# A pitch of 520 words in place of 512 for the rows of a weight ring in SBUF

## The chip, the cores and the metric

The kernel runs on one core of a Trainium2 chip. The metric is the time of one execution on the device in microseconds (us). A profile is one execution taken by the hardware profiler; its span runs from the first to the last instruction.

## The reference

One decoder layer for a sequence of 256 tokens at width 2048, in float32. Cut to what is computed:

```python
h    = rms_norm(x, ln_mix_w)
proj = h @ w_in                                   # 2048 x 9216
u_pool, q, f_logit, inp, g, gate_a, gate_b = split(proj)
y_a  = multiscale_pool(u_pool, pool_mix_w, pool_scale) @ w_branch_a
y_b  = hgrn2(q, f_logit, inp, g, lb, hgrn_norm_w) @ w_branch_b   # 8 heads, chunks of 64
x    = x + (sigmoid(gate_a) * y_a + sigmoid(gate_b) * y_b) @ w_out
u    = causal_depthwise_conv(rms_norm(x, ln_ffn_w) @ w_up, conv_w, conv_b)   # 2048 x 11008
u_gate, u_val = split(u)
x    = x + (silu(u_gate) * u_val) @ w_down        # 5504 x 2048
x    = x + sigmoid(rms_norm(x, ln_ple_w) @ w_ple_gate) * (p @ w_ple)
out  = rms_norm(x, ln_final_w)
```

## The kernel before

Nearly all the work is products of the 256 tokens with large weight matrices. A float32 product is made of three float32r ones: each operand is split into a high part (what a copy to float32r keeps) and a low part (the rest), and hi*hi + hi*lo + lo*hi is accumulated in PSUM.

**Units and the ring.** The weights stream from HBM in units of two row tiles of 128 x 512 words, 508 units in all, in the order of the stages: the projection w_in (q, f, i, g twice, the pool columns), then per 512 output columns the two gates of w_in, w_branch_a and w_branch_b (the merge), then w_out, w_up (22 chunks, the last one narrow, with a convolution behind each), w_down (43 row tiles, so that the last unit of each chunk has one), w_ple and w_ple_gate (the gate stage). Unit u goes through slot u % 4 of a ring of RING = 4 slots that three arrays share: `raw` (as it came), `w_hi` and `w_lo`. Each array is [128 partitions, 4 slots, 2 rows, 512 words].

- SP issues the DMA into `raw` (`rows`, L364; for w_up two DMAs of 2 x 256 words, L372 and L373) as soon as DVE has finished with the unit four before (`slot_split`).
- ACT copies `raw` to `w_hi` (`split_hi`, L737) three units ahead of PE (LEAD), once PE has finished the unit that held the slot.
- DVE subtracts, `w_lo` = `raw` - `w_hi` (`split_lo`, L941).
- PE takes the unit (`unit`, L504 to L518): for each of the two rows a, for each of the two blocks of 128 tokens, three matmuls. The stationary operand is 128 x 128 of the activations, the moving one is a row of the ring, 512 words.

Units of w_up's last chunk use 2 x 256 words of each row pair; in the ring copies that is five units (`width_of`).

**The stationary operands** are xT_hi and xT_lo for w_in, w_up and w_ple_gate; yaT and obT for the two branches; mT for w_out; aT for w_down; pT for w_ple. **Layout:** SBUF tensors are allocated in the order of the code: x_tok, xT_hi, xT_lo, raw, w_hi, w_lo, then ident and small vectors, then everything else. In the built program they start at these bytes of a partition: x_tok 16512, xT_hi 32896, xT_lo 49280, raw 65664, w_hi 82048, w_lo 98432, ident 114816, yaT_hi and aT_hi 119520, mT_hi 160480, dT 211424. In the changed program the first four stay; w_hi starts at 82304, w_lo at 98944, ident at 115584, yaT_hi and aT_hi at 120288, mT_hi at 161248, dT at 212192.

Between units PE has side work on the PSUM tensor `aux`: transposes (L533) and the small products of the HGRN and pool branches (L580, L604, L614). The order on each engine is written out by hand by slot number (`slot(s)` on ACT and DVE, `AUX_USES` for PE); semaphores `hi_full`, `lo_full` and `units_done` count units.

Of the kernel before, what the change touches and what calls it, by code (L numbers as in the profile page):

```python
# [33 lines left out]
F32R = mybir.dt.float32r  # L34
I32 = mybir.dt.int32

P = 128
# [15 lines left out]
NCOL = 512  # L53
NQ = D // NCOL
FW = NCOL // 2
LAST_FW = D_FF % FW
HALVES = (64, 32, 16, 8, 4, 2, 1)
LN_MIN = 2.0 ** -64
# [2 lines left out]
RING = 4  # L61
# [3 lines left out]
UD = (KF + 1) // 2  # L65
NUP = (D_FF + FW - 1) // FW
MIX = 10 * UK
# [108 lines left out]
def plus(base, per, it):  # L176

    return base if it is None else it * per + base


def build(nc, x, p, ln_mix_w, w_in, pool_mix_w, pool_scale, hgrn_lb_logits, hgrn_norm_w, w_branch_a,
          w_branch_b, w_out, ln_ffn_w, w_up, conv_w, conv_b, w_down, ln_ple_w, w_ple_gate, w_ple,
          ln_final_w, ident_c, levels_c, band_c, out):
    with ExitStack() as ctx:
        def sem(name):
            return ctx.enter_context(nc.semaphore(name))

        def sb(name, shape, dt=F32, where=ctx):
            return where.enter_context(nc.sbuf_tensor(name, shape, dt))
# [2 lines left out]
        x_tok = sb("x_tok", [P, TB, D])  # L192
        xT_hi = sb("xT_hi", [P, KD, SEQ], F32R)
        xT_lo = sb("xT_lo", [P, KD, SEQ], F32R)
        raw = sb("raw", [P, RING, 2, NCOL])
        w_hi = sb("w_hi", [P, RING, 2, NCOL], F32R)
        w_lo = sb("w_lo", [P, RING, 2, NCOL], F32R)
        ident = sb("ident", [P, P])
        vecT = sb("vecT", [P, NVEC])
        convT = sb("convT", [P, 4, 2 * KF])  # L200
# [67 lines left out]
        raw_full = [sem(f"raw_full{r}") for r in range(RING)]  # L268
# [63 lines left out]
        def width_of(u, it):  # L332


            return 2 * LAST_FW if it is None and DOWN - UK + LEAD <= u < DOWN else NCOL

        def cols(n):
            return slice(n * NCOL, (n + 1) * NCOL)
# [13 lines left out]
        @block.sync  # L352
        def _(sp):
            def slot_split(u, it=None):

                if u >= RING:
                    sp.wait_ge(lo_full, plus(u - RING + 1, 2 * UK, it))

            def rows(u, w, k, col):


                slot_split(u)
                n = min(2, w.shape[1] - k)
                sp.dma_start(raw[:, u % RING, 0:n, :], w[:, k:k + n, col:col + NCOL]).then_inc(raw_full[u % RING], 32)  # L364

            def up_unit(u, k, col, width, it=None):

                def src(c):
                    at = slice(c, c + width) if it is None else bass.ds(it * (2 * FW) + c, width)
                    return w_up_v[:, k:k + 2, at]  # L370
                slot_split(u, it)
                sp.dma_start(raw[:, u % RING, :, 0:width], src(col)).then_inc(raw_full[u % RING], 16)  # L372
                sp.dma_start(raw[:, u % RING, :, width:2 * width], src(D_FF + col)).then_inc(raw_full[u % RING], 16)  # L373

            x_v = x[0].rearrange("(b p) n -> p b n", p=P)
            sp.dma_start(mrows[:], ln_mix_w[0].rearrange("(r c) -> r c", c=P)).then_inc(const_in, 16)
            sp.dma_start(ident[:], ident_c).then_inc(const_in, 16)
            sp.dma_start(x_tok[:, :, cols(0)], x_v[:, :, cols(0)]).then_inc(x_in[0], 16)
            for u in range(4):
                rows(u, w_in_v, 2 * u, PROJ[0])  # L380
                if u < NQ - 1:
                    sp.dma_start(x_tok[:, :, cols(u + 1)], x_v[:, :, cols(u + 1)]).then_inc(x_in[u + 1], 16)
            for u in range(4, MIX):
                rows(u, w_in_v, 2 * (u % UK), PROJ[u // UK])
                if u == 14:
                    sp.dma_start(levels[:], levels_c).then_inc(late_in, 16)
                    sp.dma_start(band[:], band_c).then_inc(late_in, 16)
                    sp.dma_start(mixw[:].rearrange("p g a n -> p (g a) n"),
                                 pool_mix_w[0].rearrange("g (a p) n -> p (g a) n", p=P)).then_inc(late_in, 16)
            u = MIX  # L390
            for n in range(NQ):
                for w, k, col in ((w_in_v, UK, COL_GA), (w_in_v, UK, COL_GB), (w_a_v, UB, 0), (w_b_v, UB, 0)):
                    for i in range(k):
                        rows(u, w, 2 * i, col + n * NCOL)
                        u += 1
            for n in range(NQ):
                for i in range(UK):
                    rows(u, w_out_v, 2 * i, n * NCOL)
                    u += 1
            for i in range(UK):  # L400
                up_unit(UP + i, 2 * i, 0, FW)
            with sp.Fori(0, UP_PAIRS) as it:
                for j in (1, 2):
                    for i in range(UK):
                        up_unit(UP + j * UK + i, 2 * i, j * FW, FW, it)
            for i in range(UK):
                up_unit(DOWN - UK + i, 2 * i, (NUP - 1) * FW, LAST_FW)
            u = DOWN
            for n in range(NQ):
                for i in range(UD):  # L410
                    rows(u, w_down_v, 2 * i, n * NCOL)
                    u += 1
                    if n == 0 and i == 10:

                        sp.wait_ge(aT_ready, NUP)
                        sp.dma_start(p_tok[:], p[0, 0].rearrange("(b p) n -> p b n", p=P)).then_inc(p_in, 16)
            for n in range(NQ):
                rows(u, w_ple_v, 0, n * NCOL)
                u += 1
            for n in range(NQ):  # L420
                for i in range(UK):
                    rows(u, w_pg_v, 2 * i, n * NCOL)
                    u += 1
                    if n == 0 and i == 0:

                        sp.wait_ge(units_done, PLEW)
                        sp.dma_start(lnf[:], ln_final_w.rearrange("(a n) -> a n", a=1).to_broadcast([P, D])).then_inc(lnf_in, 16)
            out_v = out[0].rearrange("(b p) n -> p b n", p=P)
            for k in range(2):
                for tb in range(TB):  # L430

                    sp.wait_ge(y_ready[tb], k + 1)
                    half = slice(k * (D // 2), (k + 1) * (D // 2))
                    sp.dma_start(out_v[:, tb, half], x_tok[:, tb, half]).then_inc(out_done, 16)
            sp.wait_ge(out_done, 16 * 2 * TB)
# [3 lines left out]
        def _(pe):  # L439
# [81 lines left out]
            def chunk_unit(u, c, i, n, hi, lo, k, **more):  # L521
                if i == 0 and c >= 2:
                    main_released(c - 2)
                unit(u, c, i, n, hi, lo, k, **more)
                for name in AUX_AT.get(u, ()):
                    side(name)
# [178 lines left out]
            for i in range(UK):  # L705
                chunk_unit(DOWN - UK + i, C_DOWN - 1, i, UK, xT_hi, xT_lo, 2 * i, width=2 * (LAST_FW))
            u = DOWN
# [584 lines left out]
```

## Time and profile before

| | us |
|---|---|
| median of 3 runs | 1504.12 (1504.04 to 1504.55) |
| span of the profiled execution | 1502.9 |
| PE busy | 1475.8 (98%) |
| DVE busy | 871.6 (58%) |
| ACT busy | 747.7 (50%) |
| POOL busy | 125.9 (8%) |

The span is 1.2 us below the median of the runs. A matmul's busy time in the profile includes its pipeline, so matmuls overlap in the rows: the pitch, from the start of one to the start of the next, tells what one costs, and the mean duration does not. PEld, the weight load, runs beside PE. In the timeline the first column is the start, the second the duration.

### The profile page before, as it was taken

How to read it: one execution, taken by the hardware profiler on the slowest of the kernel's cores; microseconds unless marked ns; L12 is line 12 of the kernel's file. 1: busy time of each engine (PE TensorE's matmuls, PEld its weight loads, DVE VectorE, ACT ScalarE, POOL GpSimd, SP SyncE). 2: the span in 40 equal slices, each digit the busy share in tenths (PEclk: the TensorE clock that was granted, in tenths of full speed). 3: DMA queues.
4: the chain of work that ended last, by engine and by line, in shares of the span. 5: the costliest groups of instructions: out<-in, count | busy, mean ns of one | idle time of the engine just before them, and what ended most of it. 6: DMA issues, size and time to landing. Idle time of an engine off the chain costs nothing.

```text
span 1502.9 us, 18747 instructions
## 1 busy us (share of the span) xinstructions
PE 1475.8 (98%) x6814; PEld 1221.0 (81%) x6814; DVE 871.6 (58%) x968; ACT 747.7 (50%) x918; POOL 125.9 (8%) x80
## 2 busy tenths in 40 slices
PE   7999999999999999999999999999999999999996
PEld 5888888888888888888888888888888888888784
DVE  4576676445454545556676676676676455454554
ACT  5555645444444444545555555555555344343543
POOL 1033143000000000001011011010010000000000
PEclk9999999999999999999999999999999999999998
DMA  7755555456666655555655665655645655555652
GB/s 231 251 151 147 153 153 154 140 176 185 189 190 187 194 185 180 182 182 177 197 184 170 199 184 173 196 183 179 195 147 182 217 187 184 177 193 174 223 190 93
DMA packets 189466, 271.88 MB, mean 181 GB/s; under 512 B 11348, under 2 KB 103080, under 8 KB 189280
## 3 DMA queue, kind: packets, MB, share of 16 engines
q1 hardware_dynamic: 189120, 270.88, 56.9%
q8 instruction: 39, 0.64, 0.2%
q0 software_dynamic: 288, 0.21, 0.1%
q14 instruction: 19, 0.16, 0.0%
HBM read 268.95 MB, written 2.10 MB: 180 GB/s over the span
## 4 chain that ended last, share of the span: by engine, by line
PE 90%; issue 7%; DVE 1%; ACT 1%; DMA 0%; POOL 0%; POOLq 0%; ACTq 0%; SPq 0%; DVEq 0%
PE main L516 28%; PE main L518 28%; PE main L517 28%; PE aux L533 3%; PE aux L580 2%; PE aux L614 0%; DVE w_lo L941 0%; DMA x_tok<-in_x 0%; PE aux L604 0%; DVE cv L1084 0%; ACT w_hi L737 0%; DVE bT L1041 0%; POOL dec L1237 0%; ACT cv L845 0%; PE aux L593 0%
## 5 line engine op out<-in xcount | busy, mean ns | idle before, releaser
L941 DVE TENSOR_TENSOR w_lo<-raw,w_hi 128x1024 fp32r<-128x1024 f32 x508 | 651.2, 1286 | 565.7 <-ACT w_hi L737 565.3
L737 ACT ACTIVATE w_hi<-raw 128x1024 fp32r<-128x1024 f32 x508 | 536.0, 1056 | 659.1 <-PE main L518 643.5
L516 PE MATMUL main<-w_hi,xT_hi 128*128 128x512 f32 (+1 forms) x1408 | 552.1, 392 | 4.3 <-DVE w_lo L941 4.3
L518 PE MATMUL main<-w_hi,xT_lo 128*128 128x512 f32 (+1 forms) x1408 | 546.6, 388 | 0.0
L517 PE MATMUL main<-w_lo,xT_hi 128*128 128x512 f32 (+1 forms) x1408 | 546.1, 388 | 0.0
L516 PEld LDWEIGHTS main<-w_hi,xT_hi 128*128 128x128 f32 x1408 | 265.3, 188 | 57.8 <-issue 4.4
L518 PEld LDWEIGHTS main<-w_hi,xT_lo 128*128 128x128 f32 x1408 | 265.1, 188 | 54.4
L517 PEld LDWEIGHTS main<-w_lo,xT_hi 128*128 128x128 f32 x1408 | 265.4, 188 | 52.2
L516 PE MATMUL main<-w_hi,aT_hi 128*128 128x512 f32 x344 | 136.9, 398 | 0.1
L518 PE MATMUL main<-w_hi,aT_lo 128*128 128x512 f32 x344 | 136.5, 397 | 0.0
L517 PE MATMUL main<-w_lo,aT_hi 128*128 128x512 f32 x344 | 136.5, 397 | 0.0
L1247 POOL TENSOR_TENSOR act<-cv 128x512 f32<-128x512 f32 (+1 forms) x22 | 47.3, 2151 | 448.1 <-DVE cv L1084 448.1
L1084 DVE SCALAR_TENSOR_TENSOR cv<-aux,convT,cv 128x255 f32<-128x255 f32 (+1 forms) x172 | 71.2, 476 | 20.8 <-ACT cv L845 17.9
L516 PEld LDWEIGHTS main<-w_hi,aT_hi 128*128 128x128 f32 x344 | 64.9, 189 | 15.8 <-issue 0.3
L518 PEld LDWEIGHTS main<-w_hi,aT_lo 128*128 128x128 f32 x344 | 64.8, 189 | 15.7
L517 PEld LDWEIGHTS main<-w_lo,aT_hi 128*128 128x128 f32 x344 | 64.9, 189 | 15.5
L1204 POOL TENSOR_TENSOR st<-st,minus_half 128x2 f32<-128x2 f32 x4 | 4.2, 1060 | 766.4 <-DVE st L971 766.4
L516 PE MATMUL main<-w_hi,mT_hi 128*128 128x512 f32 x128 | 51.1, 399 | 0.0
L518 PE MATMUL main<-w_hi,mT_lo 128*128 128x512 f32 x128 | 50.8, 397 | 0.0
L517 PE MATMUL main<-w_lo,mT_hi 128*128 128x512 f32 x128 | 50.7, 396 | 0.0
L845 ACT ACTIVATE cv<-aux,convT 128x256 f32<-128x256 f32 x86 | 41.5, 563 | 0.5 <-PE aux L533 0.2
L1237 POOL TENSOR_TENSOR dec<-dec,qT 128x512 f32<-128x512 f32 x16 | 37.5, 2341 | 0.0
(157 smaller groups left out, 921.1 us busy)
## 6 DMA issues: line engine op xcount, KB each, us to landing
raw<-in_w_up SPq DMA_DIRECT2D x336, 256.0 KB
raw<-in_w_in SPq DMA_DIRECT2D x144, 512.0 KB
raw<-in_w_down SPq DMA_DIRECT2D x84, 512.0 KB
raw<-in_w_out SPq DMA_DIRECT2D x32, 512.0 KB
raw<-in_w_ple_gate SPq DMA_DIRECT2D x32, 512.0 KB
raw<-in_w_branch_a SPq DMA_DIRECT2D x16, 512.0 KB
raw<-in_w_branch_b SPq DMA_DIRECT2D x16, 512.0 KB
x_tok<-in_x SPq DMA_DIRECT2D x4, 512.0 KB, 8.1
```

What stands on the lines that cost most here:

```text
L516: pe.matmul(acc, th, wh, start=first, stop=False)
L517: pe.matmul(acc, th, wl, start=False, stop=False)
L518: mm = pe.matmul(acc, tl, wh, start=False, stop=end)
L533: mm = pe.transpose(dst[:, b, tb * P:(tb + 1) * P], src(b, tb), ident[:])
L580: mm = pe.matmul(flat[:, o:o + n], e[:, a:a + P], right, start=True, stop=True)
L737: ac.activation(w_hi[:, u % RING, :, 0:w], raw[:, u % RING, :, 0:w], ACT.Copy).then_inc(hi_full, 1)
L845: last_op = ac.activation(cv[:, b, :], aux_blocks(name)[:, b, :], ACT.Identity, scale=convT[:, 2, f0(f)], bias=convT[:, 3, f0(f)])
L941: dve.tensor_tensor(w_lo[:, u % RING, :, 0:w], raw[:, u % RING, :, 0:w], w_hi[:, u % RING, :, 0:w].bitcast(F32), ALU.subtract).then_inc(lo ...
L1084: last_op = dve.scalar_tensor_tensor(out=cv[:, b, d:SEQ], in0=z[:, b, 0:SEQ - d], scalar=convT[:, tap, f0(f)], in1=cv[:, b, d:SEQ], op0=AL ...
L1204: pool.tensor_tensor(dst, base, minus_half[:, 0:base.shape[1]], ALU.pow).then_inc(done, 1)
L1237: pool.tensor_tensor(e[:, :, 1, :], e[:, :, 1, :], halves(qT_flat, m)[:, :, 1, :], ALU.mult).then_inc(qk_ready, 1)
L1247: pool.tensor_tensor(act[:, 0:nf, :], cv[:, 0:nf, :], cv[:, nf:2 * nf, :], ALU.mult).then_inc(prod_u, 1)
```

## The change

Each row of `raw`, `w_hi` and `w_lo` gets 8 words (32 bytes) behind its 512. Row a of slot r then starts 2080 * (2 * r + a) bytes into its array, in place of 2048 * (2 * r + a). The three arrays grow from 16384 to 16640 bytes in a partition. All uses take the first 512 words of a row.

```diff
+PITCH = NCOL + 8
...
-        raw = sb("raw", [P, RING, 2, NCOL])
-        w_hi = sb("w_hi", [P, RING, 2, NCOL], F32R)
-        w_lo = sb("w_lo", [P, RING, 2, NCOL], F32R)
+        raw = sb("raw", [P, RING, 2, PITCH])
+        w_hi = sb("w_hi", [P, RING, 2, PITCH], F32R)
+        w_lo = sb("w_lo", [P, RING, 2, PITCH], F32R)
...
-                sp.dma_start(raw[:, u % RING, 0:n, :], w[:, k:k + n, col:col + NCOL]).then_inc(raw_full[u % RING], 32)
+                sp.dma_start(raw[:, u % RING, 0:n, 0:NCOL], w[:, k:k + n, col:col + NCOL]).then_inc(raw_full[u % RING], 32)
```

The built program has the same instructions in the same order on every engine. The ring copies on ACT and DVE change their form. DVE's first rows before:

```order
L949 SCALAR_TENSOR_TENSOR xT_lo<-aux,vecT,xT_hi 128x256 x4
L941 TENSOR_TENSOR w_lo<-raw,w_hi 128x1024 x4
L949 SCALAR_TENSOR_TENSOR xT_lo<-aux,vecT,xT_hi 128x256 x4
L941 TENSOR_TENSOR w_lo<-raw,w_hi 128x1024 x2
L949 SCALAR_TENSOR_TENSOR xT_lo<-aux,vecT,xT_hi 128x256 x4
```

and now (a line of code was added, so numbers are one higher):

```order
L950 SCALAR_TENSOR_TENSOR xT_lo<-aux,vecT,xT_hi 128x256 x4
L942 TENSOR_TENSOR w_lo<-raw,w_hi 128x2x512 x4
L950 SCALAR_TENSOR_TENSOR xT_lo<-aux,vecT,xT_hi 128x256 x4
L942 TENSOR_TENSOR w_lo<-raw,w_hi 128x2x512 x2
L950 SCALAR_TENSOR_TENSOR xT_lo<-aux,vecT,xT_hi 128x256 x4
```

Nothing moved; a run of 1024 words became two rows of 512.

## Rows read from the trace of the kernel before

**Rows 1.** The page: span, and busy time by engine (engine busy us (share) xinstructions).
```profile
span 1502.9 us, 18747 instructions
PE 1475.8 (98%) x6814; PEld 1221.0 (81%) x6814; DVE 871.6 (58%) x968; ACT 747.7 (50%) x918; POOL 125.9 (8%) x80
```

**Rows 2.** The cores: span and mean granted TensorE clock.
```profile
core 0: 1502.9 us, clock 0.997
```

**Rows 3.** The chain that ended last: its shares of the span by line.
```profile
by line: PE main L516 28.2%; PE main L518 28.1%; PE main L517 28.0%; issue 6.9%; PE aux L533 2.5%; PE aux L580 1.8%; PE aux L614 0.5%; DVE w_lo L941 0.4%; DMA x_tok<-in_x 0.3%; PE aux L604 0.2%; DVE cv L1084 0.2%; ACT w_hi L737 0.2%; DVE bT
```

**Rows 4.** The waits: who waited for whom, us in total, times, longest.
```profile
ACT w_hi L737 <- PE main L518: 643.5, 454, 2.2
...
ACT w_hi L737 <- DMA raw<-in_w_down: 8.2, 6, 3.5
...
PE main L516 <- DVE w_lo L941: 4.3, 2, 4.0
```

**Rows 5.** Timeline of PE, gate stage: first and last of 112 matmuls in a row.
```profile
1419.69 0.39 PE L518 MATMUL main<-w_hi,xT_lo 128*128 128x512 f32 x1
...
1444.85 0.39 PE L518 MATMUL main<-w_hi,xT_lo 128*128 128x512 f32 x1
```

**Rows 6.** Timeline of PE, down stage: first and last of 92 matmuls in a row.
```profile
1210.63 0.40 PE L518 MATMUL main<-w_hi,aT_lo 128*128 128x512 f32 x1
...
1231.95 0.40 PE L516 MATMUL main<-w_hi,aT_hi 128*128 128x512 f32 x1
```

**Rows 7.** Groups by line and form, L516 by its stationary tile (the second name).
```profile
L516 PE MATMUL main<-w_hi,xT_hi 128*128 128x512 f32 x1376 | 542.7, 394 | 4.0 <-DVE w_lo L941 4.0
...
L516 PE MATMUL main<-w_hi,aT_hi 128*128 128x512 f32 x344 | 136.9, 398 | 0.1
...
L516 PE MATMUL main<-w_hi,mT_hi 128*128 128x512 f32 x128 | 51.1, 399 | 0.0
...
L516 PE MATMUL main<-w_hi,yaT_hi 128*128 128x512 f32 x64 | 25.4, 397 | 0.0
```

**Rows 8.** The chain in order of time: two pieces of PE's side work.
```profile
271.36 3.45 PE aux L614 x16
...
1131.87 0.89 PE aux L533 x8
```

**Rows 9.** Groups by line and form: ring copies, and flat ones of 512 words.
```profile
L941 DVE TENSOR_TENSOR w_lo<-raw,w_hi 128x1024 fp32r<-128x1024 f32 x503 | 646.8, 1290 | 563.1 <-ACT w_hi L737 562.7
...
L737 ACT ACTIVATE w_hi<-raw 128x1024 fp32r<-128x1024 f32 x503 | 532.8, 1060 | 656.4 <-PE main L518 640.7 <-DMA raw<-in_w_down 8.2 <-DMA raw<-in_w_in 6.9
...
L1098 DVE TENSOR_TENSOR aT_lo<-act,aT_hi 128x512 f32 x20 | 13.7, 685 | 0.0
...
L854 ACT ACTIVATE aT_hi<-act 128x512 f32 x20 | 12.3, 614 | 0.0
...
L941 DVE TENSOR_TENSOR w_lo<-raw,w_hi 128x512 fp32r<-128x512 f32 x5 | 4.5, 910 | 2.6 <-ACT w_hi L737 2.6
```

**Rows 10.** The same groups, ACT's narrow ring copy.
```profile
L737 ACT ACTIVATE w_hi<-raw 128x512 fp32r<-128x512 f32 x5 | 3.2, 633 | 2.8 <-PE main L518 2.8
```

**Rows 11.** The tile w_lo: durations in ns of the ring copies, min/median/max.
```profile
L941 DVE TENSOR_TENSOR w_lo<-raw,w_hi x508: 683/1226/2322, 11.1 to 1478.4; 128x1024 fp32r<-128x1024 f32 x169, 128x512 fp32r<-128x512 f32 x1
```

**Rows 12.** Timeline, merge stage: ring copies of one slot and the next use.
```profile
448.48 1.06 ACT L737 ACTIVATE w_hi<-raw 128x1024 fp32r<-128x1024 f32 x1 [1.66 <-PE main L518]
449.57 1.23 DVE L941 TENSOR_TENSOR w_lo<-raw,w_hi 128x1024 fp32r<-128x1024 f32 x1 [1.49 <-ACT w_hi L737]
...
459.36 1.06 ACT L737 ACTIVATE w_hi<-raw 128x1024 fp32r<-128x1024 f32 x1 [1.66 <-PE main L518]
```

**Rows 13.** The page: SP's DMA queue (packets, MB, share of 16 engines' span).
```profile
q1 hardware_dynamic: 189120, 270.88, 56.9%
```

**Rows 14.** A stretch of the up stage: busy us of each engine (xinstructions), PEclk, DMA share, GB/s.
```profile
1000.00:1100.00 100.00, 100.00 (x459) 83.14 (x458) 68.90 (x85) 55.61 (x72) 11.00 (x5) 1.00 0.58 182
```

## The prediction, made before the changed kernel ran

> **What bounds the kernel now.** I read the page first, then the chain, the waits and stretches of the timeline. The page gives a span of 1502.9 us in which TensorE (PE) is busy for 98%, at full granted clock: 0.997 over the run, the higher level, 2.4 GHz [rows 1, 2]. Of the chain that ended last the three matmuls of `unit` (L516 to L518) hold 84.3% and PE's side work (L533, L580, L614, L604) 5.0%; the two ring copies, L737 on ACT and L941 on DVE, hold 0.2% and 0.4% of it [rows 3]. So the time is (matmuls) x (pitch of one), plus side work of PE, plus a start and a tail. The waits say the same from the other side: ACT waits 643.5 us for PE before its ring copies, while PE waits 4.3 us in all for a ring copy, 4.0 of it once, at the start [rows 4].
>
> The pitch is therefore the number to know. In a stretch without side work in the gate stage, 112 matmuls in a row start between 1419.69 and 1444.85 us: 25.16 / 111 = 0.2267 us each [rows 5]. In the down stage 92 in a row start between 1210.63 and 1231.95 us: 21.32 / 91 = 0.2343 us each [rows 6]. The instruction, its 512 columns, the ring behind it and the granted clock are the same. What differs is the stationary tile: xT in the first, aT in the second. **Where a tile lies in SBUF is thus worth 0.0076 us a matmul.** The layout follows from the sizes in the code, and the built program states it: x_tok, xT_hi, xT_lo, raw, w_hi and w_lo all start at a multiple of 64 bytes (at 128 past a multiple of 256), while every tile behind the small vectors (yaT, obT, mT, aT, pT) starts at 224 past a multiple of 256, so 32 past a multiple of 64. Of the 512-wide groups of L516, 1376 matmuls have xT and 344 + 128 + 64 + 64 = 600 one of the others (obT has a row like that of yaT) [rows 7]; L517 and L518 have as many. The slower pitch is paid 1800 times, 13.7 us of the span.
>
> **The change, part by part.** No instruction is added, removed or moved, no wait changes, and PE reads the same 512 words of one row per matmul. Four things do change.
>
> (1) *The moving operand's address.* Row k = 2 * slot + a of w_hi and w_lo moves by 32 * k bytes. For a = 0 the start stays at a multiple of 64; for a = 1 it comes to lie 32 past one. Half of the matmuls are of the second kind: 1376 * 3 / 2 = 2064 with xT, and 504 (aT, whose last tile of 43 has no partner) + 192 + 192 = 888 with the others, 2952 in all. The trace has no matmul of this type with a moving operand at such an offset. From above I bound it by the only price that an offset has in the trace: 2952 * 0.0076 = +22.4 us. From below, if the new offset cured the slow pairs instead of hurting, 888 * -0.0076 = -6.7 us, and -13.7 us if it cured all 1800. The nearest row for a moving operand alone is L614: 16 plain fp32 matmuls whose moving tile dT lies 32 past a multiple of 64 take 3.45 us, 0.216 us per 256 columns or 0.84 ns a column; L533, whose moving tile ident lies at a multiple of 64, takes 0.89 us for 8 of 128 columns, 0.87 ns a column [rows 8]. There the moving offset costs nothing. Those stream at half the columns per time of the kernel's main matmuls (0.2267 us / 512 = 0.44 ns a column), so the row is evidence, not proof. I take 0, since it is the one row in which a moving operand lies so.
>
> The Trainium skill, SBUF — State Buffer, section "Door 1: The DMA port swizzle", speaks of lines of 16 bytes and of a price only where consecutive accesses leave a line. A start at 32 past a multiple of 64 would by that rule be as good as any, and the sum would be 0; the pitches of [rows 5] and [rows 6] differ all the same, so here the measurement is ahead of the rule.
>
> The Trainium skill, TensorE: Matmul & The Clock Gate, section "Weight-path perf modes", says that weights that are not FP32 are read as four chunks at once over four interfaces, and its own interface is left to the stream. No row here shows the chunks. By it the offset would matter to the stationary tile and not to the moving one, which is the reading of 0 again.
>
> (2) *The stationary tiles.* Each ring array grows by 256 bytes, so all behind it moves by 256, 512 or 768. Offsets within 256 bytes stay what they were: xT fast, the others slow. 0 us.
>
> (3) *The ring copies.* L737 and L941 read and write two rows of 512 words in place of one run of 1024. The five narrow units of each already do it in two rows, of 256 words: ACT 633 ns against 614 ns for a flat 512, DVE 910 ns as a mean against 685 ns [rows 9, 10], though the shortest of the five takes 683 ns [rows 11], so that one long one makes the mean. A second row costs ACT some 20 ns and DVE from 0 to 225 ns, on copies of 1060 and 1290 ns [rows 9]. What covers it: ACT starts a ring copy as PE ends a unit, at 448.48 us, and the copy into the same slot follows at 459.36, four units on; DVE has finished the slot at 449.57 + 1.23 = 450.80 us, 2.3 us after the start [rows 12]. PE comes to that slot three units later, 3 * 12 * 0.2267 = 8.16 us after it freed it. The cover is 8.16 - 2.3 = 5.8 us per slot. On the path lie only the copies at which the ring has run empty; the chain gives them 0.2% (3 us) and 0.4% (6 us) [rows 3]. Three ACT copies at +0.02 and five DVE copies at 0 are +0.1 us; with 0.225 on the five it would be +1.2 us. I take +0.1.
>
> (4) *The DMAs.* The source runs are 2 KB (1 KB for w_up) before and after, so the number of packets stays; the destination rows start at other multiples of 32 bytes. The queue holds the 16 engines for 56.9% of the span [rows 13], and a slot's transfer is issued when DVE has finished with it (450.80 us) and wanted at 459.36 us: 8.5 us for 0.52 MB, which take 2.9 us at the 182 GB/s of a stretch of the conv stage [rows 14]. ACT does wait for raw data (8.2 us in six places of the down stage [rows 4]), but with 5.8 us to go before PE. Only the first 12 us have no cover. I take 0, and up to +1 us.
>
> **The sum:** 1502.9 + 0 + 0 + 0.1 + 0 = 1503.0 us of span, and with the 1.2 us that the median of the runs (1504.12) lies above it, **1504.2 us**.
>
> **The rivals.**
>
> *A: the moving offset costs as much as the stationary one.* The 2952 matmuls on odd rows go from 0.2267 (or 0.2343) to 0.0076 more: 1504.2 + 22.4 = 1526.6 us. This ends on the other side. For it: it is the same memory, and a 32-byte step costs in one operand already [rows 5, 6]. Against it: L614 [rows 8]. It decides from the first odd row, in every unit, and nothing hides it, since PE has no slack. Had it half the price: 1515.4.
>
> *B: what counts is the difference of the two offsets.* In the fast group both operands lie alike (128 past a multiple of 256), in the slow group they differ by 32 modulo 64; the trace can't tell this from the stationary offset alone. Then odd rows with xT become slow, 2064 * 0.0076 = +15.7 us, and odd rows with the others become fast, -6.7 us: 1513.2 us.
>
> *C: the new offset or the shifts of rows relieve the slow group,* with xT unharmed: 1504.2 - 6.7 = 1497.5 us, or 1490.5 us if all 1800 gain. For it: both ring rows and stationary tiles now lie at a common pitch (512 bytes is a divisor of both), and the change breaks that. Against it: the xT group has the same common pitch and stands at 0.2267.
>
> *D: the two-row copies or unaligned DMA rows become the bound.* DVE is the nearest: in the conv stage it is busy 68.9 us of 100 [rows 14], with 100 / 2.72 = 36.8 units in it. It would take 31.1 / 36.8 = 0.85 us more per copy before DVE is the bound, against 0.0 to 0.225 measured on two-row copies. Short of that only starts and stage borders suffer; at five times my price, 1.5 us, plus 2 us of DMA at the start, 1507.7 us.
>
> That the change does nothing at all where it is aimed is the forecast itself.
>
> **How the numbers follow.** Forecast 0.66; A 0.12 (of it 0.04 near half the price); B 0.10; C 0.08 (half of it at 1497.5); D 0.04. A measurement of this kernel can tell about 0.2% (3.0 us) from no change. Faster takes C, 0.08; same takes the forecast, 0.66; slower takes A, B and D, 0.26. The range from 1497 to 1515 us holds the forecast, B, D and half of C, 0.84; without B it would hold too little. It leaves out A at full price and the large form of C. The forecast's own range is 1503 to 1506.5.
>
> **What would show it.** Right: the pitch of the gate stage's main matmuls stays at 0.2267 and that of the down stage at 0.2343, in starts of a unit's first six matmuls (a = 0) and last six (a = 1) alike; L737 stays within 1.05 to 1.09 us and L941 near its mean; PE's wait for L941 stays under 6 us. A shows as two pitches within each unit of the gate stage, six and six; B as the same there, and the reverse order in the down stage. C shows as a down stage under 0.2343. D leaves the pitch alone and shows as PE waiting for w_lo. The forecast is wrong if any row of the main matmuls has another pitch than before; the copies and the DMAs can move by several times my prices without showing.

## The result: 17.2 us slower, and one mean pitch for all stationary tiles

The changed kernel takes **1521.3 us** (median of 4 runs, 1520.9 to 1521.6) against 1504.1 us before: ratio 1.0114, 95% interval 1.0100 to 1.0128. I had forecast 1504.2 us with a range of 1497 to 1515, so the sign of the change (none) and the range were both wrong. The profiled execution has a span of 1519.6 us, 16.7 more than before.

The page and the cores of the changed kernel, to be read beside [rows 1] and [rows 2]:

```profile
span 1519.6 us, 18747 instructions
PE 1492.3 (98%) x6814; PEld 1219.2 (80%) x6814; DVE 871.2 (57%) x968; ACT 747.8 (49%) x918; POOL 124.9 (8%) x80
```

```profile
core 0: 1519.6 us, clock 0.997
```

The same instructions, the same clock, DVE and ACT as busy as before to 0.4 us. PE alone has 16.5 us more, which is the loss. Its waits (who waited for whom: us, times, longest) answer to [rows 4]:

```profile
ACT w_hi L738 <- PE main L519: 662.0, 454, 2.1
...
ACT w_hi L738 <- DMA raw<-in_w_down: 9.0, 6, 3.5
...
PE main L517 <- DVE w_lo L942: 4.5, 3, 4.0
```

PE waits 0.2 us more for the ring than before, and ACT waits 18.5 us longer for PE. So no other engine holds PE up; its own matmuls take longer. The timeline of PE shows how much. The gate stage, first and last of 88 matmuls in a row, for [rows 5]:

```profile
1439.78 0.39 PE L517 MATMUL main<-w_hi,xT_hi 128*128 128x512 f32 x1
...
1460.00 0.40 PE L517 MATMUL main<-w_hi,xT_hi 128*128 128x512 f32 x1
```

and the down stage, again 88, for [rows 6]:

```profile
1229.65 0.40 PE L517 MATMUL main<-w_hi,aT_hi 128*128 128x512 f32 x1
...
1249.87 0.39 PE L517 MATMUL main<-w_hi,aT_hi 128*128 128x512 f32 x1
```

Both are 20.22 / 87 = 0.2324 us. The fast pitch of xT (0.2267) rose and the slow one of aT (0.2343) fell, to the same mean. Counted from the starts of all main matmuls of 512 columns that another one follows, after the first 20 us and without the few pitches above 0.3 us, the mean went from 0.2271 to 0.2324 us for xT (3994 of them) and from 0.2343 to 0.2324 us for the others (1825): 3994 * 0.00524 = +20.9 us and 1825 * -0.00186 = -3.4 us, together +17.5 us for a loss of 17.2.

What I had feared of the copies did not happen. Groups by line and form, beside [rows 9] (this view adds up the words of both rows, so that 2 x 512 stands as 128x1024 here):

```profile
L942 DVE TENSOR_TENSOR w_lo<-raw,w_hi 128x1024 fp32r<-128x1024 f32 x503 | 646.2, 1289 | 580.2 <-ACT w_hi L738 579.9
...
L738 ACT ACTIVATE w_hi<-raw 128x1024 fp32r<-128x1024 f32 x503 | 532.9, 1060 | 674.7 <-PE main L519 659.3 <-DMA raw<-in_w_down 9.0 <-DMA raw<-in_w_in 5.8
```

Two rows of 512 words cost what one run of 1024 did, 1289 against 1290 ns and 1060 against 1060 ns. The DMA queue's share fell from 56.9% to 54.9% of a longer span.

### The profile page after: what moved, and what is told of

It reads as the page before. It is cut to its first block, busy times and chain, and to the rows that moved or that the text cites. A ratio compares the mean times of both kernels' runs of the same rounds, so it can differ in the third digit from the quotient of the medians.

```text
span 1519.6 us, 18747 instructions
## 1 busy us (share of the span) xinstructions
PE 1492.3 (98%) x6814; PEld 1219.2 (80%) x6814; DVE 871.2 (57%) x968; ACT 747.8 (49%) x918; POOL 124.9 (8%) x80
## 3 DMA queue, kind: packets, MB, share of 16 engines
q1 hardware_dynamic: 189120, 270.88, 54.9%
## 4 chain that ended last, share of the span: by engine, by line
PE 90%; issue 7%; DVE 1%; ACT 1%; DMA 0%; POOL 0%; POOLq 0%; ACTq 0%; SPq 0%; DVEq 0%
PE main L517 28%; PE main L518 28%; PE main L519 28%; PE aux L534 2%; PE aux L581 2%; PE aux L615 0%; DVE w_lo L942 0%; DMA x_tok<-in_x 0%; PE aux L605 0%; DVE cv L1085 0%; ACT w_hi L738 0%; DVE bT L1042 0%; POOL dec L1238 0%; ACT cv L846 0%; PE aux L595 0%
## 5 line engine op out<-in xcount | busy, mean ns | idle before, releaser
L517 PE MATMUL main<-w_hi,xT_hi 128*128 128x512 f32 (+1 forms) x1408 | 558.4, 397 | 4.4 <-DVE w_lo L942 4.3
L518 PE MATMUL main<-w_lo,xT_hi 128*128 128x512 f32 (+1 forms) x1408 | 552.5, 392 | 0.0
```

The costliest lines, as they stand in the source:

```text
L517: pe.matmul(acc, th, wh, start=first, stop=False)
L518: pe.matmul(acc, th, wl, start=False, stop=False)
```

## The experiments

Three theories stood after the result. **Difference:** the pitch depends on how far the start of the moving row lies from that of the stationary tile, modulo some power of two (only the remainder counts). The trace of the changed kernel points to it: sorted by row of the ring, row 3 of xT and row 6 of aT both give 0.2341, 0.2350, 0.2316, 0.2398, 0.2334 and 0.2367 us in turn, within 0.0002, and rows 2 and 5 agree as well; the two tiles' starts differ by three rows' worth, 96 bytes within 256. The other six pairs of rows agree less well, by up to 0.004 us in a single one of their six pitches, so this is a pointer and not a proof. **Own offset:** each operand has a price for its own start, as I had read the trace of before. **Traffic:** the copies or DMAs, displaced, disturb PE.

### The pitch by itself, first sweep

A kernel without the layer: x is copied in and out, and PE runs sets of 24 matmuls, each with its own load, with nothing beside them. Each of the three sweeps below is a single execution, at a mean granted clock of 0.996 or 0.997. Shortened:

```python
def sweep(s, m):                       # s, m in words
    for i in range(24):
        pe.matmul(acc, stat[:, s:s + 128], mov[:, m:m + 512], start=i == 0, stop=i == 23)
    mark()                             # one matmul of 128 columns
for s in range(8):
    for m in range(8):
        sweep(8 * s, 8 * m)
...                                    # further sets: larger offsets, 4 to 16 bytes, 256 columns
```

> A kernel of its own, which computes nothing of the layer: after the copies of x it only runs float32r matmuls of 128x128 by 512 columns in sets of 24, each set with one start offset of the stationary tile and one of the moving row (both from one base, in steps of 32 bytes), while ACT, DVE and the DMAs are idle. Between two sets stands one matmul of 128 columns. Theory 1 (difference): the pitch depends only on the difference of the two offsets; equal offsets give 0.2267 us wherever they lie, and sets with the same difference modulo 256 bytes agree. Stationary 96 bytes ahead of the moving row gives 0.2343 us as in the down stage of before. Theory 2 (own offset): the stationary tile costs 0.2343 us when it lies 32 bytes past a multiple of 64, whatever the moving row does, and a moving row has a price of its own, so that rows and columns of the table add up. Theory 3 (traffic): without copies and DMAs every set gives 0.2267 us, because the extra is contention with other engines.

The timeline of PE: start, duration, and one row for each set. The four sets here have the stationary tile at 32 bytes and the moving row at 0, 32, 64 and 96.

```profile
103.89 5.80 PE L59 MATMUL main<-mov,stat 128*128 128x512 f32 x24
...
109.58 5.68 PE L59 MATMUL main<-mov,stat 128*128 128x512 f32 x24
...
115.16 5.80 PE L59 MATMUL main<-mov,stat 128*128 128x512 f32 x24
...
120.85 5.72 PE L59 MATMUL main<-mov,stat 128*128 128x512 f32 x24
```

The set with equal offsets is the shortest, and it is one in which both lie 32 bytes past a multiple of 64. The first few matmuls of a set settle in, so the pitch is the mean of the last 15 pitches. All 64 sets fall into one list by the difference (moving less stationary, modulo 256 bytes), whose values within an entry lie at most 0.0009 us apart:

| difference, bytes | 0 | 32 | 64 | 96 | 128 | 160 | 192 | 224 |
|---|---|---|---|---|---|---|---|---|
| pitch, us | 0.2269 | 0.2333 | 0.2289 | 0.2334 | 0.2325 | 0.2343 | 0.2334 | 0.2333 |

With the moving row, or the stationary tile, 256 to 480 bytes on, the same values come again, within 0.0008 us of this list. Difference 160 is the case of before in the down stage (128 less 224, modulo 256), and it has 0.2343 us here too. Traffic has fallen as the cause of the extra: it is there though nothing ran beside PE. Own offset has fallen as well: equal offsets give the fast pitch at all eight places.

### The five stationary tiles moved

```diff
         warm = sb("warm", [P, TB * 4])
+        pad = sb("pad", [P, 40])
```

> The kernel before with 160 unused bytes ahead of yaT, so that yaT, obT, mT, aT and pT start at 128 past a multiple of 256, as xT and the ring rows do. Theory 1 and theory 2 both: the 1800 slow matmuls fall from 0.2343 to 0.2267 us, 1504.1 - 13.7 = 1490.4 us. If the slow pitch has to do with the place in SBUF or with the stages and not with an offset (theory 3), it stays 1504.1 us.

Measured: **1490.9 us**, ratio 0.9910 (0.9893 to 0.9926). The timeline of the down stage, 90 matmuls in a row:

```profile
1209.70 0.39 PE L517 MATMUL main<-w_hi,aT_hi 128*128 128x512 f32 x1
...
1229.87 0.39 PE L519 MATMUL main<-w_hi,aT_lo 128*128 128x512 f32 x1
```

20.17 / 89 = 0.2266 us. The price of an offset that the prediction read from [rows 5] and [rows 6] was real, and 160 bytes of padding take it off nearly whole: 13.3 us of the 13.7 worked out. (The 13.7 leaves out pT, which lies like the others: 48 more matmuls, 0.4 us.) This kernel beats both.

With `[P, 8]`, 32 bytes, in the same place:

> The kernel before with 32 unused bytes ahead of yaT, so that these tiles start at a multiple of 256, and so of 64, but 128 bytes off the offset of the ring rows. Theory 2 (own offset, 64 bytes): as good as 160 bytes, 1490.4 us. Theory 1 (difference modulo 256): the difference is now 128 in place of 96; the rows of the changed kernel that stand 128 off xT have a pitch of 0.231 to 0.235 us, so the gain is small: 1498 to 1505 us.

Measured: 1501.1 us, ratio 0.9980 (0.9970 to 0.9989). Down stage, 87 in a row:

```profile
1209.81 0.39 PE L517 MATMUL main<-w_hi,aT_hi 128*128 128x512 f32 x1
...
1229.79 0.40 PE L519 MATMUL main<-w_hi,aT_lo 128*128 128x512 f32 x1
```

19.98 / 86 = 0.2323 us, close to the sweep's 0.2325 for 128 bytes. A start at a multiple of 256 doesn't help the tile if the ring rows lie elsewhere.

### The changed kernel with the same padding

```diff
         warm = sb("warm", [P, TB * 4])
+        pad = sb("pad", [P, 40])
```

on top of the change.

> The changed kernel with 160 unused bytes ahead of yaT, which made the kernel before 13.3 us faster. Difference theory: the eight ring rows now stand at all eight multiples of 32 bytes against every stationary tile wherever it starts, and the mean of the eight values of the sweep is 0.2319 us for each tile, so the padding does nothing here: 1521.3 us, within 2 us. Own-offset theory (the stationary tile's start costs by itself): the 13.3 us come off here too, 1508 us.

Measured: 1520.4 us, ratio 1.0107 (1.0090 to 1.0124). The padding that was worth 13.3 us before is worth 0.9 here: with eight rows at eight offsets, neither of the two places tried is a good one. Its gate stage, 88 in a row, 20.22 / 87 = 0.2324 us:

```profile
1439.71 0.39 PE L520 MATMUL main<-w_hi,xT_lo 128*128 128x512 f32 x1
...
1459.93 0.39 PE L520 MATMUL main<-w_hi,xT_lo 128*128 128x512 f32 x1
```

### One array at a time

The change on `raw` alone (w_hi and w_lo back at 512):

```diff
         raw = sb("raw", [P, RING, 2, PITCH])
-        w_hi = sb("w_hi", [P, RING, 2, PITCH], F32R)
-        w_lo = sb("w_lo", [P, RING, 2, PITCH], F32R)
+        w_hi = sb("w_hi", [P, RING, 2, NCOL], F32R)
+        w_lo = sb("w_lo", [P, RING, 2, NCOL], F32R)
```

> The change on raw alone: pitch 520 for raw, 512 for w_hi and w_lo. The DMAs and the reading side of both copies are as in the changed kernel, PE's operands as before (yaT and the others at the old offset within 256 bytes). Theory 1 and 2: 1504.1 us, within 0.1%. Theory 3 (the copies or DMAs with rows at other offsets disturb PE): at least half of the loss, 1512 us or more.

Measured: 1504.2 us, ratio 1.000 (0.9991 to 1.0010). The displaced DMA rows, and copies that read `raw` in displaced rows, cost nothing that can be measured. (Their writing side is in unbroken runs here; the run with 576 words below has `w_hi` written in separate rows, at no cost either.)

On `w_hi` alone:

```diff
-        raw = sb("raw", [P, RING, 2, PITCH])
+        raw = sb("raw", [P, RING, 2, NCOL])
...
-        w_lo = sb("w_lo", [P, RING, 2, PITCH], F32R)
+        w_lo = sb("w_lo", [P, RING, 2, NCOL], F32R)
```

> One part of the change: pitch 520 for w_hi alone, 512 for raw and w_lo. Two of three matmuls stream a row of w_hi. Difference theory: two thirds of the loss of 17.2 us, 1515.6 us. If loss came from the splitting of the copies or the shift of what lies behind: no two thirds; with only the ACT copy's writing side in rows, under 1510 us.

Measured: 1518.6 us, ratio 1.0094 (1.0077 to 1.0111), a loss of 14.4 us where two thirds would be 11.5. The gate stage, 88 in a row, 20.18 / 87 = 0.2320 us:

```profile
1439.64 0.39 PE L517 MATMUL main<-w_hi,xT_hi 128*128 128x512 f32 x1
...
1459.82 0.40 PE L517 MATMUL main<-w_hi,xT_hi 128*128 128x512 f32 x1
```

On `w_lo` alone, in the same way:

> The other part alone: pitch 520 for w_lo, 512 for raw and w_hi; one of three matmuls streams w_lo. Additive theory with the whole loss of 17.2 us and w_hi's measured 14.4 us: 2.8 us, 1507.0 us; by a third of the loss it would be 1509.9 us. Carry-over theory, by which w_hi alone took more than two thirds because a displaced matmul disturbs the next one too: more than a third here as well, 1511 to 1516 us.

Measured: 1518.9 us, ratio 1.0097 (1.0080 to 1.0113). One matmul in three displaced costs 14.8 us, as much as two in three, and above even what I expected of the carry-over. Gate stage, 88 in a row, 20.14 / 87 = 0.2315 us:

```profile
1439.72 0.40 PE L518 MATMUL main<-w_lo,xT_hi 128*128 128x512 f32 x1
...
1459.86 0.40 PE L518 MATMUL main<-w_lo,xT_hi 128*128 128x512 f32 x1
```

So the parts don't add: 14.4 + 14.8 against 17.2 for both.

### Mixed offsets and widths, by themselves

```python
o = m if other is None or i % 3 != 1 else other
pe.matmul(acc, stat[:, s:s + 128], mov[:, o:o + cols], ...)
```

> A third sweep without copies and DMAs, sets of 48. First the moving offset changes inside a set as in the real unit (two of three matmuls on a row at offset m, the third at 0; then the reverse), against sets in which all stand at m. Additive theory (each matmul has the price of its own difference): the mean of a mixed set lies at two thirds, or one third, of the way from 0.2267 us to the value of the set with all at m. Carry-over theory (a displaced matmul also disturbs the next one): the mixed sets lie above that, near the value of the full set. Then widths from 384 to 512 columns with differences of 0, 96 and 32 bytes: the first fine sweep gave no extra at 384 columns and 0.0062 us or more at 512, so it must begin between them; a stall that grows with the stream would rise in steps, a single collision would appear at once.

Sets of 48, the stationary tile fixed. The timeline of PE shows, in this order: all moving rows at 0, all at 32 bytes, all at 64; then two of three at 32 bytes and one at 0, two of three at 64; then one of three at 32, one of three at 64.

```profile
238.02 11.12 PE L60 MATMUL main<-mov,stat 128*128 128x512 f32 x48
...
249.04 11.41 PE L60 MATMUL main<-mov,stat 128*128 128x512 f32 x48
...
260.34 11.22 PE L60 MATMUL main<-mov,stat 128*128 128x512 f32 x48
```

```profile
69.58 11.41 PE L60 MATMUL main<-mov,stat 128*128 128x512 f32 x48
...
80.88 11.41 PE L60 MATMUL main<-mov,stat 128*128 128x512 f32 x48
```

```profile
159.47 11.31 PE L60 MATMUL main<-mov,stat 128*128 128x512 f32 x48
...
170.68 11.34 PE L60 MATMUL main<-mov,stat 128*128 128x512 f32 x48
```

Mean pitch over the last 30 starts: all at 32 bytes 0.2332 us, two of three 0.2334, one of three 0.2313, none 0.2267. At 64 bytes: all 0.2290, two of three 0.2334, one of three 0.2320. Two thirds and one third of the way would be 0.2310 and 0.2289, and 0.2282 and 0.2275. The additive theory has fallen: a matmul's pitch depends on its neighbours' offsets too, and a mixture can be dearer than either of its parts. It is not always dearer than the share would make it. Two of three at 128 bytes have 0.2289 us where two thirds of the way to 0.2324 would be 0.2305, and one of three at 192 bytes has 0.2289, just its share; the other mixtures lie above theirs. The means over all eight offsets are 0.2318 us for two of three and 0.2309 for one of three, and xT's matmuls have 0.2320 us in the kernel with `w_hi` alone and 0.2317 with `w_lo` alone (counted as in the result). That is how w_lo alone can cost nearly all, and why the list of the first sweep, made of uniform sets, is a guide to the kernel and not its sum.

The widths, with differences of 0 and of 96 bytes (stationary ahead), at 480, 496 and 512 columns:

```profile
410.20 10.63 PE L60 MATMUL main<-mov,stat 128*128 128x480 f32 x48
420.73 10.62 PE L60 MATMUL main<-mov,stat 128*128 128x480 f32 x48
...
441.91 10.93 PE L60 MATMUL main<-mov,stat 128*128 128x496 f32 x48
452.74 10.93 PE L60 MATMUL main<-mov,stat 128*128 128x496 f32 x48
...
474.56 11.12 PE L60 MATMUL main<-mov,stat 128*128 128x512 f32 x48
485.58 11.45 PE L60 MATMUL main<-mov,stat 128*128 128x512 f32 x48
```

Over the last 30 starts, at 480 and 496 columns the 96 bytes cost nothing (0.2165 and 0.2167 us, 0.2234 and 0.2233 us), at 512 they cost 0.0075 us; at 416 and 448 columns that set is even 0.0015 and 0.0028 us cheaper. With 32 bytes the extra is there at 480 and 496 already (0.2200 and 0.2268 us), is 0.0005 at 448 and 0.0018 at 416, and gone at 384 (0.1733 us for all three). From 496 to 512 columns the pitch with equal offsets grows by 0.0033 us where 16 columns at the rate from 480 to 496 take 0.0069. That rate would give 0.2303 us at 512: equal offsets lie 0.0036 below it, the 96 bytes 0.0039 above. About half of the gap is thus that the full width with equal offsets does better than the narrower ones.

### The offset in steps of 4 bytes

> The same kind of sweep: sets of 24 float32r matmuls of 512 columns with the moving row fixed and the stationary tile moved in steps of 4 bytes over 256 bytes, then widths of 128, 256, 384 and 512 columns with equal offsets and with the stationary tile 96 bytes ahead. No copies and no DMAs beside it. Difference theory (period 256 bytes): at the multiples of 32 bytes the values of the first sweep return (0.2267, 0.2328, 0.2333, 0.2341, 0.2323, 0.2339, 0.2293, 0.2331 us for the stationary tile 0, 32, ... 224 bytes ahead), whatever lies between. The rival, two lists of good and bad starts for each operand alone, would have given the same value for every set with a stationary start at a multiple of 64. On the widths: if the extra is a fixed stall at a matmul's start, the 96-byte difference adds 0.0076 us at each width; if it is spread over the stream, it grows with the columns, 0.0038 at 256.

Sets of 24, the moving row fixed and the stationary tile at 0, 4, 8, 12 and 16 bytes:

```profile
58.53 5.68 PE L59 MATMUL main<-mov,stat 128*128 128x512 f32 x24
...
64.11 5.79 PE L59 MATMUL main<-mov,stat 128*128 128x512 f32 x24
...
69.80 5.75 PE L59 MATMUL main<-mov,stat 128*128 128x512 f32 x24
...
75.44 5.81 PE L59 MATMUL main<-mov,stat 128*128 128x512 f32 x24
...
81.16 5.66 PE L59 MATMUL main<-mov,stat 128*128 128x512 f32 x24
```

The eight values of the first sweep came back to within 0.0008 us (again over the last 15 pitches). (Here the moving row lies at 0, so a tile 32 bytes ahead is the list's difference of 224.) Between them lies no simple staircase: with the stationary tile 16, 120, 132, 144, 156 or 240 bytes ahead the pitch is 0.2266 or 0.2267 us, as with 0; 4 bytes give 0.2326; 52 of the 64 places lie between 0.2295 and 0.2350, and the dearest, 164 bytes, gives 0.2374. No place was better than equal offsets by more than 0.0001 us. Both forms that I had expected of the widths missed: at 256 columns the 96-byte difference gave 0.1187 against 0.1200 us, less in place of more, and at 128 and 384 columns it changed nothing (0.1117 and 0.1117, 0.1734 and 0.1733).

Off the multiples of 32 bytes the difference modulo 256 is not all that counts. The first sweep also moved the row alone, by 4 and 16 bytes (the first two lines), and this one has the tile 240 and 252 bytes ahead (the last two), which are the same differences modulo 256:

```profile
512.99 5.90 PE L59 MATMUL main<-mov,stat 128*128 128x512 f32 x24
...
524.51 5.78 PE L59 MATMUL main<-mov,stat 128*128 128x512 f32 x24
```

```profile
399.69 5.70 PE L59 MATMUL main<-mov,stat 128*128 128x512 f32 x24
...
416.70 5.82 PE L59 MATMUL main<-mov,stat 128*128 128x512 f32 x24
```

At a difference of 16 bytes the row ahead gives 0.2314 us and the tile 240 ahead 0.2267; at 4 bytes it is 0.2367 against 0.2334. So the rule modulo 256 stands for multiples of 32 bytes, where all 64 pairs bear it out, and the six good places between them were found with one place of the moving row only.

### Other pitches

`w_hi` alone with rows of 576 words, which keeps all its rows at one offset within 256 bytes:

```diff
-PITCH = NCOL + 8
+PITCH = NCOL + 64
...
-        raw = sb("raw", [P, RING, 2, PITCH])
+        raw = sb("raw", [P, RING, 2, NCOL])
...
-        w_lo = sb("w_lo", [P, RING, 2, PITCH], F32R)
+        w_lo = sb("w_lo", [P, RING, 2, NCOL], F32R)
```

> One size changed: w_hi alone with a pitch of 576 words, 2304 bytes, so that its rows are no longer a power of two apart but all keep the same offset within 256 bytes. Difference theory: nothing changes, 1504.2 us. If the distance of rows as such matters (rows in other places of the memory, copies in two rows), the time moves as with 520: 1515 us or a gain.

Measured: 1504.4 us, ratio 1.000 (0.9991 to 1.0010), against 1518.6 for the same edit with 520. So it is not the distance between rows, nor that it leaves a power of two, but the offset within 256 bytes. Gate stage, 107 in a row, 24.03 / 106 = 0.2267 us:

```profile
1419.77 0.39 PE L517 MATMUL main<-w_hi,xT_hi 128*128 128x512 f32 x1
...
1443.80 0.39 PE L518 MATMUL main<-w_lo,xT_hi 128*128 128x512 f32 x1
```

All three arrays with 528 words, every row at a multiple of 64:

```diff
-PITCH = NCOL + 8
+PITCH = NCOL + 16
```

> One size changed: pitch 528 words for all three arrays, 64 bytes more than 512 words, so that every ring row starts at a multiple of 64, at four different places within 256 bytes. Difference theory: against xT the differences 0, 64, 128, 192 bytes have in the sweep a mean of (0.2267 + 0.2294 + 0.2323 + 0.2334) / 4 = 0.2305 us, against the others 0.2333 us: 4224 * 0.0037 - 1800 * 0.0010 = +13.9 us, 1518 us. Own-offset theory, in which a start at a multiple of 64 is as good as any other: 1504 us.

Measured: 1522.2 us, ratio 1.0119 (1.0102 to 1.0136). Own offset is wrong by 18 us. The difference list, taken as a sum, is 4 us short (the 4224 in it should be 1376 * 3 = 4128, which makes it 0.4 us less still); that fits the carry-over, and no run shows it by itself for these offsets. Gate stage, 88 in a row, 20.19 / 87 = 0.2321 us, where the four uniform values have a mean of 0.2304:

```profile
1441.66 0.40 PE L517 MATMUL main<-w_hi,xT_hi 128*128 128x512 f32 x1
...
1461.85 0.40 PE L517 MATMUL main<-w_hi,xT_hi 128*128 128x512 f32 x1
```

## Why the prediction was wrong

**What bounds the kernel** held: matmuls times pitch, nothing else on the path. So did the reading that a tile's place is worth 0.0076 us; the padded kernel collected it.

**The step that failed is (1), the moving operand's address.** The sum had 0 us for it; it came to +17.5 us, counted from the pitches. It had two faults. The first is the value taken: 0, on the strength of L614 [rows 8], a plain fp32 matmul of 256 columns at half the rate. The sweeps show that even among float32r matmuls the width decides: at 256 and 384 columns a difference of 96 bytes costs nothing, and L614 is 256 wide. What is more, its two operands lie alike: by the layout dT starts at 211424 and mixw, the stationary one, 4096 bytes behind it, both 224 past a multiple of 256. The row has the good pair of offsets and could show nothing of an unequal one. A row of another type, width and pair could not stand for this one, and I had called it evidence and not proof, and then let it carry 0.66 of the chance. The second fault is the model behind the bounds. I set apart odd rows (32 past a multiple of 64) from even ones and left the even rows at their old pitch; the period is 256 bytes, and seven of eight rows were displaced. In the changed kernel xT's mean pitch rose over all rows, even ones included (row 2, 64 bytes off: 0.2289 us; row 4, 128 bytes off: 0.2329), and even row 0, whose offset is still equal, has 0.2313 us, between displaced ones. The thought that the offset matters to the stationary tile alone fell with it: in the first sweep the row moved by 32 bytes with the tile at rest goes from 0.2267 to 0.2333 us.

**Rival B** named the right cause: the difference of the two offsets counts, xT loses and the others gain. It was mis-sized, since it counted the difference modulo 64 and each matmul by itself. It had +0.0076 us on 2064 matmuls (+15.7) and -0.0076 on 888 (-6.7), 1513.2 us. What happened is +0.0052 on nearly all with xT (+20.9) and -0.0019 on nearly all the others (-3.4). The others didn't return to the fast pitch on any large part, since equal offsets are one case in eight, and a mixture spoils that one too (row 3 of aT, with equal offsets now, has 0.2315 us). **Rival A** (1526.6) had a larger total by the wrong mechanism: under it the padding would have helped the changed kernel.

**The signs to look for** were partly wrong with it: neither A's "six and six" nor B's appeared, since no row kept its old pitch. "Wrong if any row of the main matmuls has another pitch" was the one that told.

**(2), (3) and (4)** held. (2): the other tiles' own offsets within 256 bytes did not change. (3) and (4): raw alone at 520 gives 1504.2 us. The copies were even cheaper than my +0.1 us.

The range held B's 1513.2 us, but not what lies between B and A: 1526.6 stood in the text as the upper bound of the unknown cost, and the range ended at 1515, because one row had set the chance of the forecast too high.

## What to carry to other kernels

In a kernel bound by back-to-back float32r matmuls of 512 columns, start the stationary tiles and the moving rows at the same offset within 256 bytes, and make the distance between rows of a ring a multiple of 256 bytes; here 160 bytes of padding behind some small vectors were worth 13.3 us of 1504. Padding a row by a few words "to spread it" does the opposite. When a trace shows one instruction at two pitches, ask what differs in the pair of operands, not in one of them, also in a row that you take as evidence, and don't cost an effect of the full width from a narrower matmul.

## What the runs showed of the hardware

- The pitch of float32r matmuls of 512 columns, each with its own load of a 128 x 128 stationary tile, is 0.2267 us with equal offsets (up to 0.2275 in one set) and 0.229 to 0.234 us with other multiples of 32 bytes, with no other engine running. For multiples of 32 bytes it depends on the difference modulo 256 bytes, not on where either lies (64 pairs, within 0.0009 us). Off them it doesn't: 0.2314 us with the row 16 bytes ahead, 0.2267 with the tile 240 ahead.
- It isn't symmetric: 64 bytes one way gives 0.2289 us, the other way (192) 0.2334.
- The prices of mixed differences don't add. Most mixtures of one offset with 0 cost more than their share, up to more than the dearer of the two (0.2334 against 0.2290 and 0.2267); two of three at 128 bytes cost less (0.2289 against 0.2305).
- The extra depends on the width: at 96 bytes none (or less than none) from 128 to 496 columns, 0.0075 us at 512.
- Plain fp32 transposes of 128 columns (`aux<-ident,z_tok`) have a median pitch of 0.109 us with a difference of 160 bytes (before) and of 0 (the kernel with 160 bytes of padding).
- Why this is so (whether the load of the next tile and the stream of the row meet in the memory) is not shown; the loads' own duration, 188 or 189 ns in the groups of both kernels, did not change. No run had a matmul without a load beside it.
